# A streaming-encoder block on one core: a third unit of the eight-unit down pairs goes by the 7-product scheme, and both ends of the program are rewritten

## What is computed

```python
h = h + 0.5 * swiglu(rms_norm(h, ffn1_norm[i]), ffn1_w_gate[i], ffn1_w_up[i], ffn1_w_down[i])
# mixer: forgetting attention, gated linear attention, gates, w_out
h = h + 0.5 * swiglu(rms_norm(h, ffn2_norm[i]), ffn2_w_gate[i], ffn2_w_up[i], ffn2_w_down[i])
ple_gate = jax.nn.sigmoid(rms_norm(h, ple_norm[i]) @ w_ple_gate[i])
h = h + ple_gate * (p[i].astype(h.dtype) @ w_ple_proj[i])
return rms_norm(h, final_norm)
```

## Time and profile before

| | us |
|---|---|
| median of 3 runs | 2199.97 (2199.21 to 2201.32) |
| the profiled execution, its own time | 2200.43 |
| its span, first to last instruction | 2198.7 |
| PE busy | 2181.5 (99%), 9811 matmuls |
| DVE busy | 1593.2 (72%) |
| ACT busy | 1125.8 (51%) |
| granted TensorE clock | 0.999 |

### The profile page before, as it was taken

The page is one execution under the profiler, slowest core; times in us unless marked ns, Lnnn a source line. Parts: engine busy times, 40 slices in busy tenths (PEclk is TensorE's granted clock), DMA queues, the critical chain, the costliest instruction groups (busy, mean ns, idle before and its releaser), DMA issues.

```text
span 2198.7 us, 24431 instructions
## 1 busy us (share of the span) xinstructions
PE 2181.5 (99%) x9811; PEld 1798.1 (82%) x9811; DVE 1593.2 (72%) x1636; ACT 1125.8 (51%) x1187; POOL 40.0 (2%) x71
## 2 busy tenths in 40 slices
PE   9999999999999999999999999999999999999998
PEld 7888888888888888877777888888888888888786
DVE  5887889878887544445655665889778987888755
ACT  6554555554555544454444545455545555455554
POOL 0000000000000200010110000000000000000000
PEclk9999999999999999999999999999999999999999
DMA  8655655655554766665555666664565565655464
GB/s 310 220 178 181 240 190 176 222 183 202 198 207 143 208 194 194 174 181 170 170 173 158 186 188 182 225 212 159 209 230 179 192 222 183 205 201 201 138 216 144
DMA packets 147003, 425.68 MB, mean 194 GB/s; under 512 B 10680, under 2 KB 10688, under 8 KB 132560
## 3 DMA queue, kind: packets, MB, share of 16 engines
q1 hardware_dynamic: 145136, 419.21, 57.7%
q0 software_dynamic: 1472, 4.70, 0.8%
q10 hardware_dynamic: 288, 0.30, 0.0%
HBM read 422.06 MB, written 2.11 MB: 193 GB/s over the span
## 4 chain that ended last, share of the span: by engine, by line
PE 96%; DVE 2%; issue 1%; ACT 1%; DMA 0%; SPq 0%; ACTq 0%; POOLq 0%; POOL 0%; DVEq 0%
PE acc L1626 11%; PE acc L1628 11%; PE acc L1627 11%; PE acc L1583 11%; PE acc L1585 10%; PE acc L1584 10%; PE turn L1626 5%; PE turn L1628 5%; PE turn L1627 5%; PE fox L1626 4%; PE fox L1628 4%; PE fox L1627 4%; PE turn L1603 1%; DVE w_lo L1158 0%; PE acc L1620 0%
## 5 line engine op out<-in xcount | busy, mean ns | idle before, releaser
L1102 DVE TENSOR_TENSOR w_lo<-raw,w_hi 128x1024 fp32r<-128x1024 f32 x275 | 343.2, 1253 | 334.8 <-ACT w_hi L663 334.7
L663 ACT ACTIVATE w_hi<-raw 128x1024 fp32r<-128x1024 f32 x275 | 290.7, 1060 | 386.3 <-PE acc L1585 366.6
L1583 PE MATMUL acc<-w_hi,x_both 128*128 128x512 f32 x768 | 303.6, 395 | 0.0
L1585 PE MATMUL acc<-w_hi,x_both 128*128 128x512 f32 x768 | 299.4, 390 | 0.0
L1584 PE MATMUL acc<-w_lo,x_both 128*128 128x512 f32 x768 | 299.0, 389 | 0.0
L1583 PEld LDWEIGHTS acc<-w_hi,x_both 128*128 128x128 f32 x768 | 144.2, 188 | 34.4 <-issue 5.7
L720 ACT ACTIVATE w_hi<-raw 128x2048 fp32r<-128x2048 f32 x62 | 118.8, 1920 | 98.8 <-DVE more L1172 33.8
L1585 PEld LDWEIGHTS acc<-w_hi,x_both 128*128 128x128 f32 x768 | 144.1, 188 | 30.7
L1584 PEld LDWEIGHTS acc<-w_lo,x_both 128*128 128x128 f32 x768 | 144.3, 188 | 28.8
L720 ACT ACTIVATE more_r<-lo_raw 128x2048 fp32r<-128x2048 f32 x61 | 116.6, 1920 | 81.2 <-DVE more L1172 43.6
L1158 DVE TENSOR_TENSOR raw_r<-raw,w_hi 128x2048 fp32r<-128x2048 f32 x62 | 141.5, 2287 | 18.4 <-ACT w_hi L720 18.0
(11 more groups left out here) (497 smaller groups left out, 5058.4 us busy)
## 6 DMA issues: line engine op xcount, KB each, us to landing
raw<-in_w_in SPq DMA_DIRECT2D x96, 512.0 KB
lo_raw<-in_ffn_up SPq DMA_DIRECT2D x43, 1024.0 KB, 4.9
raw<-in_ffn_up SPq DMA_DIRECT2D x40, 1024.0 KB, 4.9
raw<-in_w_merge_gate SPq DMA_DIRECT2D x64, 512.0 KB
raw<-in_ffn_w_down SPq DMA_DIRECT2D x29, 1024.0 KB, 5.1
more<-in_ffn_up SPq DMA_DIRECT2D x28, 1024.0 KB, 4.9
lo_raw<-in_ffn_w_down SPq DMA_DIRECT2D x26, 1024.0 KB, 5.2
raw<-in_ffn_up SPq DMA_DIRECT2D x40, 512.0 KB, 3.8
```

The lines of the kernel that those rows point to most:

```text
L663: nc.scalar.activation(w_hi[:, slot, :, :], raw[:, slot, :, :], ACT.Copy).then_inc(hi_split, 1)
L1102: nc.vector.tensor_tensor(w_lo[:, slot, :, :], raw[:, slot, :, :], w_hi[:, slot, :, :].bitcast(F32), ALU.subtract).then_inc(lo_split, 1)
L1583: nc.tensor.matmul(to, hi(kt)[:, tok], w_hi[:, slot, k, :], start=kt == 0, stop=False)
L1585: last = nc.tensor.matmul(to, lo(kt)[:, tok], w_hi[:, slot, k, :], start=False, stop=kt == BK * nb - 1)
```

## The change

Down pairs of parts 0 and 1 get a third shared unit (`HS` = 3, and `down_shared` gives 2 for part 2). Its activation sum cannot all be made where the two were: sum 0 stays two stages before the down pair, sum 1 moves there too (at `sum_made_at(i) + 3`, split one item later), and sum 2 takes the place of sum 1 in the stage before the down pair. For sum 2 there is no full-precision copy of the hidden tile (`FULL` = 2 of them), so DVE adds high part and rest first. At the start, `x_part` comes before `split`. At the end the mean square of three of the four column blocks is made ahead, DVE scales column block 1 in ACT's place, and ACT issues two of the last four stores.

```diff
-US, HS = 3, 2
+US, HS = 3, 3
+FULL = 2
...
-    return US if PAIR[i].kind == "up" else HS
+    return US if PAIR[i].kind == "up" else down_shared(PAIR[i].part)
+
+def down_shared(part):
+    return HS if PARTS[part] == 4 else HS - 1
...
-        hid_full = slab[:, 2 * HID + 8:2 * HID + 12, :, :].rearrange("p (u a) b c -> p u a (b c)", u=HS)
+        hid_full = slab[:, 2 * HID + 4 * HS:2 * HID + 4 * HS + 4, :, :].rearrange("p (u a) b c -> p u a (b c)", u=FULL)
...
-            for t in range(TT):
-                for n in range(2):
-                    for ready, c in ((out_ready_act, n), (out_ready_dve, 2 + n)):
-                        sp.wait_ge(ready, 2 * t + n + 1)
-                        columns = slice(COLS * c, COLS * (c + 1))
-                        sp.dma_start(out_tm[:, t, columns], h[:, t, columns]).then_inc(stored, 16)
+            for c, ready, count in ((2, out_ready_dve, 1), (0, out_ready_act, 1), (3, out_ready_dve, 2), (1, out_ready_dve, 3)):
+                sp.wait_ge(ready, count)
+                store(0, c)
+            sp.wait_ge(out_ready_dve, 4)
+            store(1, 2)
+            sp.wait_ge(out_ready_dve, 5)
+            store(1, 3)
...
+                        if i + 1 in LAST_UP and k == sum_made_at(i) + 4 and shared_units(name, i + 2) == HS:
+                            split_sums(name, i + 2, 1)
                         if i in LAST_UP and k == 3:
-                            split_sums(name, i + 1, 1)
+                            split_sums(name, i + 1, shared_units(name, i + 1) - 1)
...
             for j in range(1, FIRST_BLOCKS):
-                split(b + j, j % RING, j // RING + 1)
                 if j % 2 == 0:
...
                     x_part(BK * unit + 1)
+                split(b + j, j % RING, j // RING + 1)
...
-                for c in (0, 1):
-                    nc.scalar.activation(h[:, t, COLS * c:COLS * (c + 1)], embedding[:, c, t, :], ACT.Copy,
-                                         scale=rstd[:, t:t + 1]).then_inc(out_ready_act, 1)
+                nc.scalar.activation(h[:, t, 0:COLS], embedding[:, 0, t, :], ACT.Copy, scale=rstd[:, t:t + 1])\
+                    .then_inc(out_ready_act, 1)
+            act.wait_ge(out_ready_act, TT)
+            act.dma_start(out_tm[:, 1, 0:COLS], h[:, 1, 0:COLS]).then_inc(stored, 16)
+            act.wait_ge(out_ready_dve, 3 * TT)
+            act.dma_start(out_tm[:, 1, COLS:2 * COLS], h[:, 1, COLS:2 * COLS]).then_inc(stored, 16)
...
-                if PAIR[pair].kind == "up":
+                if PAIR[pair].kind == "up" or u >= FULL:
                     full, kts = m5_copy.rearrange("p (k c) -> p k c", k=2), slice(BK * u, BK * (u + 1))
...
+                        if i + 1 in LAST_UP and k == sum_made_at(i) + 3 and shared_units(name, i + 2) == HS:
+                            make_sums(name, i + 2, 1)
                         if i in LAST_UP and k == 2:
-                            make_sums(name, i + 1, 1)
+                            u = shared_units(name, i + 1) - 1
+                            make_sums(name, i + 1, u, slab_r[:, 0:HID, :], slab_r[:, HID:2 * HID, :])
...
+            dve.wait_ge(sumsq_done, 16 + 3)
+            after_own(nc.vector.tensor_reduce(meansq[:], sumsq[:, :, 0:3], AX_X, ALU.add))
+            nc.vector.tensor_scalar(meansq[:], meansq[:], 1.0 / D, EPS, ALU.mult, ALU.add).then_inc(means_begun, 1)
...
-                after_own(nc.vector.tensor_reduce(meansq[:, t:t + 1], sumsq[:, t, :], AX_X, ALU.add))
-                nc.vector.tensor_scalar(meansq[:, t:t + 1], meansq[:, t:t + 1], 1.0 / D, EPS, ALU.mult, ALU.add)\
-                    .then_inc(final_means, 1)
+                nc.vector.tensor_tensor(meansq[:, t:t + 1], meansq[:, t:t + 1], sumsq[:, t, 3:4], ALU.add).then_inc(final_means, 1)
                 dve.wait_ge(final_rstds, t + 1)
-                for c in (2, 3):
+                for c in (2, 3, 1):
```

More of the change, by code:

```diff
@@ L233, in sum_number @@
     def sum_number(name, pair, u):
-        first = (US + HS * len(PARTS)) * (name == "ffn2")
-        return first + u if PAIR[pair].kind == "up" else first + US + HS * PAIR[pair].part + u
+        first = (US + sum(down_shared(part) for part in range(len(PARTS)))) * (name == "ffn2")
+        return first + u if PAIR[pair].kind == "up" else first + US + sum(down_shared(n) for n in range(PAIR[pair].part)) + u
     x_tm = x[0].rearrange("(t p) d -> p t d", p=P)
@@ L338, in build @@
         s_lo = room_r[:, 3:6, :].rearrange("p u (s c) -> p u s c", s=4)
-        hid_hi = slab_r[:, 2 * HID:2 * HID + 4, :].rearrange("p (u a) (b c) -> p u (a b) c", u=HS, b=2)
-        hid_lo = slab_r[:, 2 * HID + 4:2 * HID + 8, :].rearrange("p (u a) (b c) -> p u (a b) c", u=HS, b=2)
-        hid_full = slab[:, 2 * HID + 8:2 * HID + 12, :, :].rearrange("p (u a) b c -> p u a (b c)", u=HS)
+        hid_hi = slab_r[:, 2 * HID:2 * HID + 2 * HS, :].rearrange("p (u a) (b c) -> p u (a b) c", u=HS, b=2)
+        hid_lo = slab_r[:, 2 * HID + 2 * HS:2 * HID + 4 * HS, :].rearrange("p (u a) (b c) -> p u (a b) c", u=HS, b=2)
+        hid_full = slab[:, 2 * HID + 4 * HS:2 * HID + 4 * HS + 4, :, :].rearrange("p (u a) b c -> p u a (b c)", u=FULL)
         m1_copy, m5_copy = room[:, 6, :], room[:, 7, :]
@@ L421, in build @@
         final_rows, final_squares = sem("final_rows"), sem("final_squares")
-        final_means, final_rstds = sem("final_means"), sem("final_rstds")
+        means_begun, final_means, final_rstds = sem("means_begun"), sem("final_means"), sem("final_rstds")
         out_ready_act, out_ready_dve, stored = sem("out_ready_act"), sem("out_ready_dve"), sem("stored")
@@ L523, in _, with store @@
                         plain(BLOCK["ple"] + first + j, w_ple_gate, BK * P * j, COLS * c)
-            for t in range(TT):
-                for n in range(2):
-                    for ready, c in ((out_ready_act, n), (out_ready_dve, 2 + n)):
-                        sp.wait_ge(ready, 2 * t + n + 1)
-                        columns = slice(COLS * c, COLS * (c + 1))
-                        sp.dma_start(out_tm[:, t, columns], h[:, t, columns]).then_inc(stored, 16)
+            def store(t, c):
+                columns = slice(COLS * c, COLS * (c + 1))
+                sp.dma_start(out_tm[:, t, columns], h[:, t, columns]).then_inc(stored, 16)
+            for c, ready, count in ((2, out_ready_dve, 1), (0, out_ready_act, 1), (3, out_ready_dve, 2), (1, out_ready_dve, 3)):
[5 more added lines that the diff above has]
+            store(1, 3)
             sp.wait_ge(stored, 16 * 4 * TT)
@@ L749, in turn_hidden @@
                     kt, bank = PAIR[pair].kt0 + 2 * ct, banks_of(name, pair)[2 * ct][:, :].rearrange("p (k c) -> p k c", k=2)
-                    if kt < BK * HS:
+                    if kt < BK * FULL:
                         nc.scalar.activation(hid_full[:, kt // BK, :, :], bank, ACT.Copy)
@@ L1077, in _ @@
                 act.wait_ge(final_rows, t + 1)
-                nc.scalar.activation(turn_bank[t][:, :], h[:, t, 3 * COLS:], ACT.Square,
+                nc.scalar.activation(turn_bank[t][:, :], h[:, t, 3 * COLS:], ACT.Square, scale=D ** -0.5,
                                      accum_out=sumsq[:, t, 3:4]).then_inc(final_squares, 1)
@@ L1292, in _ @@
             for j in range(1, FIRST_BLOCKS):
-                split(b + j, j % RING)
                 if j % 2 == 0:
@@ L1298, in _ @@
                     x_part(BK * unit + 1).then_inc(turned_lo, 1)
+                split(b + j, j % RING)
             mean_square(0)
@@ L1547, in _ @@
             splits(b, 31, 36)
+            dve.wait_ge(sumsq_done, 16 + 3)
+            after_own(nc.vector.tensor_reduce(meansq[:], sumsq[:, :, 0:3], AX_X, ALU.add))
+            nc.vector.tensor_scalar(meansq[:], meansq[:], 1.0 / D, EPS, ALU.mult, ALU.add).then_inc(means_begun, 1)
+            dve.wait_ge(means_begun, 1)
             for t in range(TT):
```

## The result

The changed kernel takes **2205.73 us** (median of 10 runs, 2203.57 to 2206.28), the kernel before 2200.09 on the same chip. The ratio is 1.0024, with a 95% interval of 1.0016 to 1.0032: **slower by 5.6 us**, and outside the range of the prediction. The profiled execution took 2205.95 us, its span 2204.2 against 2198.7.

The account below looks back on a forecast made before the run. PE, busy 99% of the span, was taken as the bound. Terms -5.4 - 0.8 - 0.5 + 2.2 + 2.2 + 1.4 + 1.2 = +0.3 us on the profiled 2200.4, less 0.5 to the median: 2200.2 us, range 2196.5 to 2203.5.

Parts of the forecast that it names:

- Matmuls removed: Eight down pairs of both nets: 24 matmuls fewer on PE at 0.227 us each, -5.4 us.
- Loads at the slot left out: PE waits for late loads: ffn1 pair 4 +2.2, ffn2 pair 3 +2.2, ffn2 pair 10 +1.4 us.
- that upper bound: The three load waits together were bounded between 5.3 and 6.6 us.
- Rival 3, the clock: Three new PE waits bring 1.2 GHz, 12 slow matmuls per wait: 8.2 us more, 2208.4; chance 0.02.
- My sign for this rival: Whole run: the prediction counts as wrong if the clock is under 0.99.
- Sum 1 moved: Pairs 2 and 8 of both nets: PE waits 0.3 us at A1, four times, +1.2 us.
- Idle time at the combine of pairs 3 and 9: DVE's idle time before the combine shrinks from 2.23 to 0.7 us, still cover.
- Start: Block 2, x first: PE can begin at 13.74 instead of 14.58, -0.8 us.
- End: Last half: shorter mean square and first store waiting for DVE instead of ACT, -0.5 us.
- Rival 1: Loads at the left-out slots arrive in time: 2194.5 us, faster; chance 0.13.
- Rival 2: Loads at the three places land 2.4 us later still: +7.2 us, 2207.4; chance 0.05.

Follow-up runs that it names:

- Kernel 5: The changed kernel with sum 1 made one item after sum 0, before DVE idles for ACT, and its rest one item later; 2201.81 us.
- kernel 1: The changed kernel with the slots left out at items 27, 59 and 91 instead of 30, 60 and 90; 2195.45 us.
- kernels 5 and 10: 10: changed kernel, slots moved, sum 1 earlier, A0's differences made ahead of the turned tiles in pair 15; 2191.02 us. For 5 see Kernel 5.
- kernel 6: Kernel 5 with a slot left out at the A2 item in each of 15 stages, for fifteen long waits; 2236.14 us.

## Why the prediction was wrong

The places of the three long waits were right, and so was what makes PE wait there: a load behind its slot. What failed is what such a wait costs. The span grew by 5.5 us where the sum has 0.3. Of the 5.2 us between them 3.2 are the clock, for which the sum has no term, 1.1 are the long waits (0.8 longer in all, and 0.11 behind each), and 0.9 the four moved sums; the start and the end gave 0.3 more than forecast, and 0.3 are in none of the terms. Step by step:

- *Matmuls removed*, -5.4: right. Pairs 5 and 11 of both nets, where nothing else changed, became 3.4 us shorter (44.88 to 41.48): 15 matmuls fewer in the stage itself, while the stage before it has the 12 of the third A item.
- *Loads at the slot left out*, +2.2, +2.2, +1.4: the waits came where they were put and measured 2.39, 2.72 and 1.49. An A item needs 10.5 and 10.8 us from the free slot, not 10.3, because the load took longer to land (5.36 and 5.68 us to DVE's first difference, not 5.14). I had this as a bound, at 0.3 each, and the three together, 6.6, are that upper bound.
- *Rival 3, the clock*, chance 0.02: **the step that failed.** I let the forecast's waits of 2 us cost only themselves, because the waits of the trace before, 1.3 us the longest that I counted, left no mark. (Two more, of 1.4 and 1.5 us, lie in its first 7 us.) A wait of 1.3 us says nothing of one of 2.4. Of rival 3's price, 8.2 us, 3.2 came true in the profiled execution: 16 slow matmuls for two waits, where it had 36 for three, and 0.2 us for each, where it had 0.227; in each of two others there were 8. At full clock the time would have been some 3.2 us shorter, 2202.5, within my range. The clock alone, on top of a sum that was otherwise right, would have given 2203.4, just inside it; with the undersized waits as well the time left it. My sign for this rival was blunt too: a mean clock under 0.99. With 16 slow matmuls it is 0.998, so it has to be read stretch by stretch. The page cited there names the effect, and I gave it almost no chance.
- *Sum 1 moved*, +1.2: too small. The four stages grew by 0.52 to 0.55 us, 2.15 in all. The waits themselves are 0.39 to 0.42 us, not 0.3. I counted the margin from the end of DVE's split to PE's start as if it could be used up to zero: PE begins 0.05 us after DVE ends, and its next matmul comes another 0.11 late. Kernel 5 shows that the term was avoidable.
- *Idle time at the combine of pairs 3 and 9*, 0.7 us forecast: DVE is idle 0.87 us in all four stages, here in pair 9 of ffn1:

```profile
400.36 0.69 DVE L1197 TENSOR_TENSOR room<-fox,room 128x512 f32<-128x512 f32 x1 [0.87 <-ACT room L745]
```

- *Start*, -0.8: PE's first matmul of block 2 at 13.57 instead of 14.58, -1.0:

```profile
12.20 2.55 DVE L1118 TENSOR_TENSOR w_lo<-raw,w_hi 128x1024 fp32r<-128x1024 f32 x2 [0.59 <-ACT w_hi L674]
...
13.57 0.47 PE L1650 MATMUL acc<-w_hi,x_both 128*128 128x512 f32 x1 [0.25 <-DVE w_lo L1118]
```

- *End*, -0.5: from the start of PE's last matmul to the end of the span 9.23 us instead of 9.78. Nearly all of it lies ahead of the first store; from that to the span's end it was 4.6 us and is 4.5 now. No gain of the second queue shows; for most of that time the DMA engines move some 350 to 420 GB/s in either kernel:

```profile
2199.66 0.81 SPq L532 DMA_DIRECT2D out<-h  x2
...
2199.96 0.38 ACTq L1098 DMA_DIRECT2D out<-h  x1
2200.46 0.39 ACTq L1100 DMA_DIRECT2D out<-h  x1
```

- *Rival 1*, loads in time, 2194.5: not what the change did, but what it does once the table of slots fits it (kernel 1, 2195.45). *Rival 2*, loads 2.4 us later still: they were 0.2 to 0.5 us later.

## What to carry to other kernels

When a new wait of PE comes out of a sum, price the clock as well: here a wait up to 1.8 us cost its length and 0.1 us, and one of 2.0 to 3.1 us cost another 1.5 to 1.6 us in 10 of 23 cases. A margin of 10.9 us against a need of 10.3 depends on a table, here the order of slots, that suited the old order of items; when an item changes its kind, the table has to be gone through again, and that was worth 10 us, more than the change's own gain of 5.4. When an engine idles and then has work that others wait for, time is gained by putting some of that work in front of the idle stretch (kernels 5 and 10), and none by changing its order behind it (the kernel that split S4 first).

## What the runs showed of the hardware

- The clock falls at single waits of PE of 2.0 to 3.1 us in a stream that is otherwise dense, in some cases: behind both of the changed kernel's in one profile, behind one of two in each of two others and in kernel 5, behind five of fifteen in kernel 6. The shortest wait with a fall is 2.13 us (kernel 6), the longest without one 3.02 us (the changed kernel's second profile). Behind waits of 1.05 to 1.78 us there was none in fifteen.
- Once down, it stays for 7 or 8 matmuls of 128x512, start to start 0.427 us against 0.227, and comes back while PE works on; a fall costs 1.5 to 1.6 us. It need not start at the wait's end: in pair 4 of ffn1 the first slow distance comes one matmul behind the waiting one in the first profile and six behind it in the second, and in pair 3 of ffn2 four behind it.

```profile
1557.47 0.50 PE L1650 MATMUL acc<-more_r,slab_r 128*128 128x512 f32 x1 [2.56 <-DVE w_lo L1174]
1557.81 0.40 PE L1651 MATMUL acc<-w_lo,slab_r 128*128 128x512 f32 x1
...
1558.54 0.63 PE L1651 MATMUL acc<-w_lo,slab_r 128*128 128x512 f32 x1
1558.96 0.63 PE L1652 MATMUL acc<-more_r,slab_r 128*128 128x512 f32 x1
```

- What decides whether a given wait brings a fall stays open. That it changes between executions of one program is shown, and so is that the place of the fall behind one and the same wait changes with them; no run here says by what.
